# A hybrid encoder layer on one core: in the rwkv stage each pair projects k before r and v, and GpSimd's low parts wait for set places

## What is computed

```python
prev = concatenate([shift0, p[:, :-1]], axis=1)
ps = p + (prev - p) * mu
r, k, v, xw, xa, xg = split(ps, RW_SPLITS, axis=-1)
w = -softplus(-(w0 + tanh(xw) @ w2)) - 0.5
decay = exp(-exp(w))
a = sigmoid(a0 + xa @ a2)
g = sigmoid(xg) @ g2
kk = hd(k * k_k)
kk = kk / maximum(sqrt(sum(kk * kk, axis=-1)), 1e-12)
k = hd(k * (1.0 + (a - 1.0) * k_a))
bonus = sum(r_h * k * r_k, axis=-1) * v_h
```

## Time and profile before

| | |
|---|---|
| median of 3 runs | 5068.87 us (5064.38 to 5071.78) |
| profiled execution | 5072.53 us, span of its instructions 5070.7 us |
| TensorE busy | 4757.4 us, 94% |
| VectorE busy | 3011.3 us, 59% |
| GpSimd busy | 2258.6 us, 45% |
| ScalarE busy | 1412.1 us, 28% |
| mean granted TensorE clock | 0.965 |

### The profile page before, as it was taken

One profiled execution on the slowest core, in us unless ns is written; L12 is line 12 of the kernel. 1 busy time (PEld: TensorE's weight loads), 2 busy tenths in 40 slices (PEclk: granted clock), 3 DMA queues, 4 the chain that ended last, 5 costly groups with the idle time before them and its releaser, 6 DMA issues. The chain is left out here.

```text
span 5070.7 us, 90897 instructions
## 1 busy us (share of the span) xinstructions
PE 4757.4 (94%) x35388; PEld 4575.4 (90%) x35388; DVE 3011.3 (59%) x4666; ACT 1412.1 (28%) x1816; POOL 2258.6 (45%) x878
## 2 busy tenths in 40 slices
PE   6999989999999989969998989999999999999998
PEld 5999888888888889969998879999999999999997
DVE  4333255555555633345877856647777777777775
ACT  3333322222212221122233323323332333333332
POOL 3222222121211123334443235547877777777873
PEclk8999999999999999989999999999999999999999
DMA  6999733333323366962233365538888878888883
GB/s 233 334 340 338 277 104 128 118 128 119 104 86 108 108 197 209 352 239 91 99 113 143 143 222 188 160 121 301 292 303 290 306 285 305 292 299 298 293 303 126
DMA packets 343249, 1077.07 MB, mean 212 GB/s; under 512 B 99344, under 2 KB 153104, under 8 KB 263952
## 3 DMA queue, kind: packets, MB, share of 16 engines
q1 hardware_dynamic: 291264, 783.02, 44.9%
q0 software_dynamic: 36864, 268.45, 14.2%
q10 hardware_dynamic: 14928, 22.84, 1.2%
HBM read 876.90 MB, written 197.29 MB: 212 GB/s over the span
## 5 line engine op out<-in xcount | busy, mean ns | idle before, releaser
L154 POOL TENSOR_TENSOR wlo<-raw,whi 128x2048 fp32r<-128x2048 f32 x170 | 792.0, 4659 | 2141.7 <-ACT whi L150 2141.7
L168 POOL TENSOR_TENSOR wlo<-raw,whi 128x1024 fp32r<-128x1024 f32 x432 | 1042.1, 2412 | 503.3 <-ACT whi L164 495.4
L164 ACT ACTIVATE whi<-raw 128x1024 fp32r<-128x1024 f32 x432 | 458.1, 1060 | 1041.2 <-PE psS L236 409.4
L236 PE MATMUL accs<-xh,whi 128*128 128x272 f32 x2624 | 581.6, 303 | 69.6 <-DMA at_before<-in_cst 40.6
L2147 DVE SCALAR_TENSOR_TENSOR Y<-R,HD,Y 128x2048 f32<-128x2048 f32 x127 | 460.2, 3624 | 217.5 <-DMA R<-in_v,IDX 212.0
L236 PE MATMUL accs<-xh,wlo 128*128 128x272 f32 x2624 | 548.9, 291 | 0.0
L236 PE MATMUL accs<-xl,whi 128*128 128x272 f32 x2624 | 548.5, 291 | 0.0
L236 PEld LDWEIGHTS accs<-xh,whi 128*128 128x128 f32 x2624 | 420.8, 192 | 93.1 <-issue 58.8
L236 PE MATMUL psS<-hh,wlo 128*128 128x416 f32 x1408 | 497.0, 353 | 0.0
L236 PE MATMUL psS<-hh,whi 128*128 128x416 f32 x1408 | 495.1, 352 | 0.0
L236 PE MATMUL psS<-hl,whi 128*128 128x416 f32 x1408 | 492.9, 350 | 0.0
(11 more groups left out here) (397 smaller groups left out, 9746.4 us busy)
## 6 DMA issues: line engine op xcount, KB each, us to landing
raw<-in_u SPq DMA_DIRECT2D x128, 1024.0 KB, 5.0
raw<-in_v SPq DMA_DIRECT2D x128, 1024.0 KB, 5.8
raw<-in_w_in SPq DMA_DIRECT2D x82, 1024.0 KB, 8.0
at_UI<-in_u SPq DMA_DIRECT2D x64, 1024.0 KB, 8.9
u_d<-at_UO SPq DMA_DIRECT2D x256, 256.0 KB, 6.2
g_d<-STG SPq DMA_DIRECT2D x8, 3328.0 KB, 10.3
Ge<-g_d SPq DMA_DIRECT2D x64, 416.0 KB, 8.4
wo_UI<-in_u SPq DMA_DIRECT2D x24, 1024.0 KB, 9.1
```

Source lines behind the costliest of these rows:

```text
L154: pool.tensor_tensor(self.lo[:, c % 2, :], self.raw[:, c % 2, :], self.hi[:, c % 2, :].bitcast(F32), ALU.subtract).then_inc(self.split_don ...
L164: act.activation(self.half(self.hi, c, h), self.half(self.raw, c, h), ACT.Copy).then_inc(self.hi_done, 1)
L168: pool.tensor_tensor(self.half(self.lo, c, h), self.half(self.raw, c, h), self.half(self.hi, c, h).bitcast(F32), ALU.subtract).then_inc(se ...
L236: mm = pe.matmul(out, w(k), x(k, n), start=a, stop=z)
```

## The change

The order of the three projections becomes k, r, v. TensorE's small(3) stands in the second unit instead of the third. ScalarE squares k behind the first unit's copy and makes the exponentials after it. VectorE mixes k first, then does the scan, the products of k up to `AA`, the second four transposes, the clip of k's sums, and only then mixes r, with `BV` as scratch instead of `T1`. GpSimd waits before three of its low parts: before unit 2 for step 6 of `rw_prep` (the subtraction behind the scan), before unit 3 for step 14 (`AR` from `RM` and `PP`), before unit 4 for the sixth count of `rw_s_free` of the pair, which `BV` gives.

```diff
         def unit_src(u, i):
-            k = 24 + 8 * u + i if u < 3 else 58 + (u - 3) + 3 * i
+            k = 24 + 8 * (1, 0, 2)[u] + i if u < 3 else 58 + (u - 3) + 3 * i
...
                 for u in range(UNITS):
+                    if u == 2:
+                        pool.wait_ge(S["rw_prep"], NPV * i + 6)
+                    if u == 3:
+                        pool.wait_ge(S["rw_prep"], NPV * i + 14)
+                    if u == 4:
+                        pool.wait_ge(S["rw_s_free"], NS * i + 6)
                     W.split_lo(pool, BASE + u, UNITS, i)
...
-                run(r)
-                run(project(BASE + 1, UNITS, i))
-                v = project(BASE + 2, UNITS, i)
-                for _ in range(8):
-                    next(v)
+                run(k)
+                r = project(BASE + 1, UNITS, i)
+                for _ in range(8):
+                    next(r)
                 pe.wait_ge(S["rw_square"], 2 * i + 1)
                 small(3, headones[:, :], lambda s: T1[:, s]).then_inc(S["rw_n2"], 1)
-                run(v)
+                run(r)
+                run(project(BASE + 2, UNITS, i))
...
-                evacuate(2, UNITS, i, shift(0))
+                evacuate(2, UNITS, i, shift(1))
                 W.split_hi(act, 4, UNITS, i)
-                act.wait_ge(S["rw_prep"], NPV * i + 5)
+                act.wait_ge(S["rw_prep"], NPV * i + 4)
+                act.activation(T1[:, :], KM[:, 0:E], ACT.Square, scale=col("k_k")).then_inc(S["rw_square"], 1)
+                act.wait_ge(S["rw_prep"], NPV * i + 6)
...
-                evacuate(3, UNITS, i, shift(1))
+                evacuate(3, UNITS, i, shift(0))
                 W.split_hi(act, 5, UNITS, i)
-                act.wait_ge(S["rw_prep"], NPV * i + 9)
-                act.activation(T1[:, :], KM[:, 0:E], ACT.Square, scale=col("k_k")).then_inc(S["rw_square"], 1)
                 act.wait_ge(S["rw_s_free"], NS * i + 5)
                 act.activation(T1[:, :], T1[:, :], ACT.Sqrt).then_inc(S["rw_decay"], 1)
+                act.wait_ge(S["rw_prep"], NPV * i + 13)
                 evacuate(4, UNITS, i, shift(2))
...
-                dve.wait_ge(S["rw_stored"], 64 * i + 16)
-                mix(ch, RM, col("mu_r"), bass.ds(i, 1), 3 * i + 3)
+                mix(ch, KM, col("mu_k"), bass.ds(8 + i, 1), 3 * i + 3, T1)
+                k, b = KM[:, 0:E], BB[:, 0:E]
+                ch(dve.memset(KM[:, E - 1:E], 0.0))
...
-                for c in range(4, 8):
-                    R.turn(dve, c, i)
-                mix(ch, KM, col("mu_k"), bass.ds(8 + i, 1), 3 * i + 4)
-                k, b = KM[:, 0:E], BB[:, 0:E]
-                ch(dve.memset(KM[:, E - 1:E], 0.0))
                 ch(dve.tensor_scalar(T2[:, :], k, col("k_k"), None, ALU.mult))
                 dve.wait_ge(S["rw_s_free"], NS * i + 3)
                 ch(dve.tensor_tensor(b, T2[:, :], AA[:, :], ALU.mult))
                 ch(dve.tensor_scalar(AA[:, :], AA[:, :], 1.0, col("k_a"), ALU.subtract, ALU.mult))
+                for c in range(4, 8):
+                    R.turn(dve, c, i)
                 dve.wait_ge(S["rw_n2"], i + 1)
                 dve.tensor_scalar(both(T1[:, :]), psS[:, :, 0:EH], 1e-24, None, ALU.max).then_inc(S["rw_s_free"], 1)
                 ch(dve.scalar_tensor_tensor(k, AA[:, :], 1.0, k, ALU.add, ALU.mult))
+                dve.wait_ge(S["rw_stored"], 64 * i + 16)
+                mix(ch, RM, col("mu_r"), bass.ds(i, 1), 3 * i + 4, BV)
```

More of the change, by code:

```diff
@@ L803, in small @@
                     return mm
-                r = project(BASE, UNITS, i)
+                k = project(BASE, UNITS, i)
                 for _ in range(11):
-                    next(r)
+                    next(k)
                 pe.wait_ge(S["lw_loaded"], 16 * i + 16)
@@ L811, in _ @@
                 for _ in range(2):
[L812 removed]
+                    next(k)
                 small(1, LW[CH:P, 0, :], lambda s: TWA[CH:P, s]).then_inc(S["rw_lora"], 1)
                 for _ in range(2):
[L815 to L821 removed]
+                    next(k)
+                small(2, LW[:, 1, :], lambda s: SGG[:, s]).then_inc(S["rw_lora"], 1)
+                run(k)
+                r = project(BASE + 1, UNITS, i)
+                for _ in range(8):
+                    next(r)
                 pe.wait_ge(S["rw_square"], 2 * i + 1)
                 small(3, headones[:, :], lambda s: T1[:, s]).then_inc(S["rw_n2"], 1)
[L824 removed]
+                run(r)
+                run(project(BASE + 2, UNITS, i))
                 advance(5)
@@ L1091, in _, with mix @@
             dve.wait_ge(S["rw_cst"], 64)
-            def mix(ch, dst, mu, at, ready):
+            def mix(ch, dst, mu, at, ready, spare):
                 dve.wait_ge(S["rw_p_ready"], ready)
-                ch(dve.tensor_tensor(T1[:, :], EX[:, 0:E], EX[:, 1:E + 1], ALU.subtract))
-                ch(dve.scalar_tensor_tensor(dst[:, 0:E], T1[:, :], mu, EX[:, 1:E + 1], ALU.mult, ALU.add))
+                ch(dve.tensor_tensor(spare[:, :], EX[:, 0:E], EX[:, 1:E + 1], ALU.subtract))
+                ch(dve.scalar_tensor_tensor(dst[:, 0:E], spare[:, :], mu, EX[:, 1:E + 1], ALU.mult, ALU.add))
                 ch(dve.tensor_copy(SH[:, at, :], EX[:, SEQ:E:DEC + 1]))
             first = Chain(dve, S["rw_first"], 6, 0)
-            mix(first, RM, par[:, C_MUWA:C_MUWA + 1], slice(24, 25), 1)
-            mix(first, KM, par[:, C_MUG:C_MUG + 1], slice(25, 26), 2)
+            mix(first, RM, par[:, C_MUWA:C_MUWA + 1], slice(24, 25), 1, T1)
+            mix(first, KM, par[:, C_MUG:C_MUG + 1], slice(25, 26), 2, T1)
             dve.wait_ge(S["rw_twa"], 3)
```

## The result

The changed kernel takes 4994.92 us (median of 4 runs, 4990.33 to 4999.74), the kernel before beside it 5070.32 us (4 runs, 5064.38 to 5072.03): a ratio of 0.9853, 95% interval 0.9836 to 0.9871, 75 us faster. The forecast was 4986 us, a gain of 83.

The account below looks back on a forecast made before the run. TensorE, busy 94%, was taken as bound, with gaps of 3.4 and 3.1 us a pair behind ScalarE's square and VectorE's `BV`; 68 and 15 us off 5072.5 give 4989.5, the median 3.7 lower: 4986 us, range 4974 to 5016.

Parts of the forecast that it names:

- The chain on VectorE: VectorE's work in each pair up to `BV`: the transposes behind it start 8.5 us earlier, 68 us in all.
- The reciprocal isn't held: VectorE's reciprocal beside GpSimd's unit 3 low part keeps its 3.57 us; rival of a held one: 5015 us, chance 0.05.
- The new wait of 0.8 us: TensorE waits about 0.8 us a pair for unit 3's low part, ahead of the gates' first unit.
- The clock: The piece from `BV`'s start to L1176 runs at full TensorE clock, 10.4 us a pair: 15 us gained in all.
- The late high part: ScalarE's unit 4 high part, its load issued later, stays hidden with 1.2 to 3.6 us slack; rival of lateness: chance 0.06.
- The sum: Whole kernel: 68 us from VectorE's chain and 15 us from the clock give 83 us, so 4986 us.
- not removed, it moves: VectorE's hold beside unit 2's low part moves from the scan to `BB`, which ends 0.58 us behind GpSimd.
- The rival of more gain: GpSimd and VectorE run tighter; the 0.8 us wait and some gaps between pairs go too: 4977 us, chance 0.08.

Follow-up runs that it names:

- third comparison: The unchanged file of the changed kernel, run a third time beside the kernel before on another chip: 4992.4 us, ratio 0.9833.
- Turns first: Changed kernel with VectorE's second four transposes directly behind the scan's subtraction: 4989.95 us, ratio 0.9843; in its second run 4989.13 us, 0.9826.
- gap filled: Turns first with one step of the gates' projection moved on TensorE ahead of the first state update: 4981.49 us, ratio 0.981 to the kernel before.
- unit 3's wait a step later: Changed kernel with GpSimd's wait before unit 3 at step 15, the reciprocal's end, instead of step 14: 5047.4 us, ratio 0.9951 to the kernel before.

## Why the prediction was right

- **The chain on VectorE: 8.5 us a pair.** In the fourth pair it is 8.6 (39.53 to 30.92 us). In the frame of before (27.22 us added) the scan starts at 1095.58 (predicted 1095.6), `BB` ends at 1103.34 (1103.5), the reciprocal starts at 1113.29 (1113.45), the product ends at 1118.56 (1118.65), `BV` starts at 1124.22 (1124.3), and the first transpose at 1125.10 (1125.1). Every term stands within 0.2 us. Over the eight pairs the chain is 67.0 us shorter, where the sum had 68.
- **The reciprocal isn't held.** It takes 3.57 us, all but the first 0.1 of it beside GpSimd (1086.17 to 1090.76). The experiment that moves GpSimd one step later shows what the place is worth: 50 us. The rule of the Trainium skill (SBUF — State Buffer, Who interferes with whom) held in every timeline: what was held had two SBUF inputs, the reciprocal and the transposes were not held (3.57 and 1.20 to 1.25 us in all thirteen profiles, beside GpSimd or not). What the Trainium skill says there of a tensor_scalar in a 2-port mode fits the trace too: GpSimd's row that starts beside `T2` takes 4.89 us instead of 4.59. It changed nothing in the sum, since `BB` behind `T2` is held either way.
- **The new wait of 0.8 us** for unit 3's low part is 0.66, and the bonus sums come at 1121.91 in the old frame (predicted 1121.9).
- **The clock: 15 us.** The stretch takes 10.58 us where I worked out 10.4, eight times; 98.1 less 84.6 is 13.5 us. The small waits that are left don't lower it there. Chain and piece make 80.5 of the stage's 82.7 us. Of the other 2.2, 1.9 lie between L1176 (now L1183) and the next pair's chain: that stretch took 92.98 us behind the sixth pair before, the one with the lowest clock in the earlier trace rows, and 90.9 to 91.3 in the others; no such pair is left. The prediction had put nothing there.
- **The late high part** came as put: 2.1 us late on ScalarE, 3.6 us of slack behind it.
- **The sum.** 83 us for the stage, against 82.7, 82.2 and 82.9 in the three profiles of the changed kernel, each against the one profile of the kernel before. The medians fell by 75, 73 and 83 us. The 8 us that are missing from the first are not in the stage. The two profiled executions differ by 77.5 us: 82.7 from the stage, less 2.0 because it starts later and less 3.2 behind the second norm; between the three profiles of the same changed kernel the start of the stage moves from 606.2 to 608.8 us and the part from the second norm's reciprocal to the last one's from 2806.3 to 2814.3 us (before: 606.5 and 2811.1). Those parts are the same in both kernels and scatter by about as much, so no step of the sum explains 4994.92 against 4986. The kernel before scatters too: in the third comparison its nine runs lie between 5063.88 and 5088.77 us. So the 83 us of that comparison, the forecast's own figure, are luck as much as the 73 of the second.
- **What the prediction didn't separate.** It told of the change as one chain. The experiments part it: the waits of units 3 and 4 carry nearly all of it, the order of k, r and v by itself 16 us (3.4 beside the waits), unit 2's wait nothing. That last followed from its own words, a hold that is "not removed, it moves".
- **The rival of more gain** named the 0.8 us and the gaps between pairs. Turns first took away the first, and gap filled another gap of 0.8 us, ahead of the state update, that the prediction had not named. With both the stage is 10 us shorter than the changed kernel's, about what this rival had put (9 us); the gaps between pairs are still there (10.5 us in all before, 10.8 in gap filled, as waits on `issue`).

## What to carry to other kernels

When two engines hold each other up, don't look for a place where neither works: look for instructions of the one that the other doesn't hold (here a reciprocal and transposes), and let the other wait for the step just ahead of them. Check that the consumer's due time still fits; one step later cost 50 us of the stage here. A wait by itself is worth only what it takes from the path: take each away alone before you believe in it, and once the bound has moved to TensorE, count its own gaps of 0.8 us before shortening another engine's chain further.

## What the runs showed of the hardware

- VectorE can hold GpSimd too, for less. In the rwkv stage of the thirteen profiles a low part takes 4.5 to 4.6 us where VectorE is idle as it starts, 4.57 to 4.60 beside a reciprocal and 4.52 to 4.67 beside transposes. Where a VectorE instruction with two SBUF inputs is at work as it starts, it is longer by about what that one has still to run: with v's subtraction 4.55, 4.73, 4.83, 5.04 and 5.16 us for 0.15, 0.32, 0.42, 0.62 and 0.73 us still to run, and 4.91 for 0.54 us of `T2`'s product with the reciprocal. `T2` itself, a tensor_scalar of 0.51 us with one SBUF input tensor, does the same: 4.88 to 4.90 for 0.45 us. The prediction had left open whether `T2` or GpSimd goes first; `T2` does.
- The granted clock isn't set by a wait alone: in one kernel, at one place, with the same 4.2 us of 5 busy and the same wait of 0.80 us ahead, it was 0.68 or 0.69 in five pairs and 1.00 in three, and at the same place in a second run 1.00 in seven. The waits between the pairs show the same: behind three of them (1.78, 1.82 and 1.86 us, one each in the kernel without unit 2's wait, in turns first's second run and in gap filled) it was 0.66 over 5 us, behind another of 1.78 us (unit 3's wait a step later) 1.00. What decides it stayed open. A stretch of the first kind makes a pair about 1.4 us longer (133.0 against 131.6), one of the second about 2 (132.9 against 130.9).
